# Two-layer pooling, attention and mixture-of-experts backbone on one core: conditioning sections summed by VectorE and GpSimd, tokens loaded first, one load held back

## What is computed

```python
for l in range(DEPTH):                        # DEPTH = 2
    m = jax.nn.silu(c) @ ada_w[l] + ada_b[l]  # ada_w[l] is 1024 x 6144
    sh1, sc1, g1, sh2, sc2, g2 = jnp.split(m, 6, axis=-1)
    if l == 0:                                # the context has a vector of its own
        mc = jax.nn.silu(c_ctx) @ ada_w[l] + ada_b[l]
        hc = modulate(rms_norm(ctx, norm1_g[l]), csh1, csc1)
    h = modulate(rms_norm(x, norm1_g[l]), sh1, sc1)
    if l == 0:
        z = h @ mix_w_in                      # 1024 x 928: pooling | queries | keys
        attn = latent_attention(q, k, v, k_c, v_c)          # 8 heads
        y = concat([multiscale_pool(z), attn]) @ mix_w_out
    else:
        y = conformer_conv(h)
    x = x + g1 * y
    h2 = modulate(rms_norm(x, norm2_g[l]), sh2, sc2)
    x = x + g2 * expert_choice_moe(h2)        # 16 experts, 64 tokens each
return rms_norm(x, final_g)
```

## Time and profile before

| | |
|---|---|
| time of 3 runs | 1566.99 us median (1566.47 to 1567.52) |
| the profiled execution | 1568.4 us, its span 1566.5 us |
| TensorE busy | 1438.4 us, 92% of the span |
| VectorE, ScalarE, GpSimd busy | 27%, 15%, 4% |
| DMA | 501.40 MB, mean 320 GB/s |
| mean granted TensorE clock | 0.971 |

### The profile page before, as it was taken

The page is one execution under the profiler, slowest core; times in us unless marked ns, Lnnn a source line. Parts: engine busy times, 40 slices in busy tenths (PEclk is TensorE's granted clock), DMA queues, the critical chain, the costliest instruction groups (busy, mean ns, idle before and its releaser), DMA issues.

```text
span 1566.5 us, 15305 instructions
## 1 busy us (share of the span) xinstructions
PE 1438.4 (92%) x5889; PEld 597.7 (38%) x5889; DVE 425.6 (27%) x867; ACT 229.5 (15%) x469; POOL 70.2 (4%) x151
## 2 busy tenths in 40 slices
PE   4999999997999899899999999997999998999996
PEld 2564555553333333333323444453433323323332
DVE  2113667333121221121113423535012111111113
ACT  3224333111110010010003112221100100100001
POOL 1000000000000000000000300001000000000001
PEclk7999999997999999999999999998999999999999
DMA  9725686148999999999999103229999999999995
GB/s 348 296 98 185 216 295 241 68 154 316 419 407 420 427 427 429 428 428 428 423 421 369 65 0 128 88 83 364 388 426 396 427 428 428 428 428 428 424 421 212
DMA packets 77234, 501.40 MB, mean 320 GB/s; under 512 B 7624, under 2 KB 8671, under 8 KB 48638
## 3 DMA queue, kind: packets, MB, share of 16 engines
q1 hardware_dynamic: 69952, 485.22, 75.8%
q0 software_dynamic: 2304, 8.39, 1.4%
q10 hardware_dynamic: 4926, 7.04, 1.3%
HBM read 494.32 MB, written 6.31 MB: 320 GB/s over the span
## 4 chain that ended last, share of the span: by engine, by line
PE 70%; DMA 21%; DVE 5%; issue 1%; ACT 1%; ACTq 1%; SPq 0%; POOL 0%; POOLq 0%; DVEq 0%
PE PS L1016 31%; DMA ring<-in_exp_wg_dram 11%; PE PS L814 7%; PE PS L1048 6%; DMA ring<-in_exp_wu_dram 5%; PE PS L733 4%; PE PS L682 4%; PE PS L845 4%; DMA ring<-in_exp_wd_dram 3%; PE PS L653 3%; PE PS L887 3%; PE PS L665 2%; PE PS L908 1%; PE PS L829 1%; PE PS L822 1%
## 5 line engine op out<-in xcount | busy, mean ns | idle before, releaser
L1016 PE MATMUL PS<-ring,arena 128*64 128x512 f32 x2880 | 673.9, 607 | 41.3 <-DMA ring<-in_exp_wg_dram 19.5
L1016 PEld LDWEIGHTS PS<-ring,arena 128*64 128x64 f32 x2880 | 220.4, 139 | 463.2 <-issue 423.6
L1708 DVE TENSOR_TENSOR x<-x,PS 128x512 f32<-128x512 f32 x128 | 87.9, 687 | 466.9 <-PE PS L1048 466.9
L1048 PE MATMUL PS<-arena 128*128 128x512 f32 x256 | 141.5, 641 | 3.7 <-DVE arena L1735 3.2
L814 PE MATMUL PS<-ring,hT 128*128 128x512 f32 x256 | 113.9, 600 | 0.0
L1339 ACT ACTIVATE arena<-PS 128x512 f32<-128x512 f32 x32 | 17.4, 594 | 467.4 <-PE PS L1016 467.4
L1735 DVE SCALAR_TENSOR_TENSOR arena<-PS,arena,g_row 128x512 f32<-128x512 f32 x32 | 22.6, 746 | 219.5 <-PE PS L1016 219.5
L1048 PEld LDWEIGHTS PS<-arena 128*128 128x128 f32 x256 | 38.3, 188 | 105.4 <-issue 97.3
L653 PE MATMUL PS<-ident,arena 128*128 128x128 f32 (+5 forms) x393 | 54.5, 278 | 25.8 <-DVE arena L1726 17.9
L814 PEld LDWEIGHTS PS<-ring,hT 128*128 128x128 f32 x256 | 48.7, 193 | 59.8 <-issue 59.0
L665 PE MATMUL PS<-ring,cond 128*32 128x512 f32 x384 | 51.8, 673 | 14.8 <-DMA ring<-in_ada_w_dram 13.9
(11 more groups left out here) (180 smaller groups left out, 1059.8 us busy)
## 6 DMA issues: line engine op xcount, KB each, us to landing
ring<-in_exp_wg_dram SPq DMA_DIRECT2D x62, 2048.0 KB, 16.1
ring<-in_exp_wd_dram SPq DMA_DIRECT2D x62, 2048.0 KB, 19.2
ring<-in_exp_wu_dram SPq DMA_DIRECT2D x56, 2048.0 KB, 17.9
ring<-in_ada_w_dram SPq DMA_DIRECT2D x24, 2048.0 KB, 9.8
ring<-in_conv_w_pw_dram SPq DMA_DIRECT2D x6, 2048.0 KB, 19.5
hT<-in_exp_wu_dram SPq DMA_DIRECT2D x4, 2048.0 KB, 15.6
ring<-in_mix_w_out_dram SPq DMA_DIRECT2D x2, 2048.0 KB, 16.6
arena<-in_exp_wu_dram SPq DMA_DIRECT2D x2, 2048.0 KB, 7.3
```

Source lines behind the costliest of these rows:

```text
L1016: last = nc.tensor.matmul(PS[64 * e:64 * e + 64, bank + half, :], lhs[:, k, 64 * e:64 * e + 64], w[e][:, half * N:(half + 1) * N], start=k ...
L1048: nc.tensor.matmul(PS[:, 6 + i % 2, :], hot[:, (i // 2) * 128:(i // 2 + 1) * 128], y_rows[:, (i % 2) * N:(i % 2 + 1) * N], start=True, sto ...
L1708: v.tensor_tensor(part, part, PS[:, 6 + i % 2, :], ALU.add).then_inc(scat_added, 1)
```

## The change

Seven things change together.

1. **Tokens first.** SyncE loads x and the context before any granule of `ada_w`; the transposes stand ahead of section 0; small vectors that layer 0's first norm does not need move from ScalarE's queue to SyncE's, behind `mix_w_in` and the pooling tables (the five rows of `params` ahead of `mix_w_in`). The first section waits for two small loads only (`first_bias_in`). `keep_warm(3)` stands before each block of section 1.
2. `cond` holds silu(c) in column 0, silu(c_ctx) in column 16 and zeros elsewhere, instead of 16 copies of each. Column 16 is cleared before attention.
3. **Early sections 2 and 3 on VectorE** (`early_terms`): granules 4 to 7 are no longer multiplied by TensorE; VectorE makes the product and the sum over the eight parts, one `tensor_scalar` and seven `scalar_tensor_tensor` of 128 x 512 per granule, after the items in `SUMMED`. The sum over the 128 partitions is left to the turn and to a `tensor_reduce` over 512 values (`section_total`) in place of 32.
4. Section 2 is turned before the pooling products, in place of after the values.
5. **Half of each late section on GpSimd**: the first granule stays with TensorE, the second is scaled in place by eight `tensor_scalar` (`scale_late`) and summed by seven `tensor_tensor` (`add_late`) into `ada_rows[:, 1]`. A third late slot is used, in turns for the second granules.
6. The loads of one late section are issued together: SyncE waits for the first granule's block of the head before, then issues both.
7. **Held load.** The ninth granule of each mixture also waits for the first gathered rows (`rows_in[0]`), and `keep_warm(6)` becomes `keep_warm(4)`.

Cut to the core:

```diff
+    o = [("xT", (k,), "VS"[k % 2]) for k in range(K8)]
+    o += [("cT", (k,), "VS"[k % 2]) for k in range(K8 // 2)]
+    o += conditioning(0) + conditioning(1)
...
+    o += conditioning(2)[2:]
     o += [("band", (0,), "V"), ("band", (1,), "V"), ("poolw", (0,), "S"), ("poolw", (1,), "S"),
...
+    return o + conditioning(3)[2:]
+SUMMED = {4: ("zlat", 1), 5: ("zlat", 2), 6: ("sel", 2, 1), 7: ("value", 2)}
...
+                    sp.wait_ge(rows_in[0], 16 * (PAIRS // 2 * l + 1))
...
+            for h in range(LATE):
                 for b in range(2):
+                    g = G_LATE + b * (1 + h % 2)
+                    if h < 1 + b:
+                        slot_free(g)
+                    elif b:
+                        sp.wait_ge(late_sum, LATE_STEPS * (h - 1))
+                    else:
+                        sp.wait_ge(late_filled, h)
+                    l, s = divmod(EARLY + h, SECTIONS // 2)
+                    sp.dma_start(slot(g).rearrange("p (k n) -> p k n", k=K8), ada_blocks(l)[s, b, :, :, :])\
+                      .then_inc(slot_in[g % SLOTS], 16)
...
+                    if args[0] in (2, 3):
+                        keep_warm(3)
...
+                    if args[0] in (2, 3):
+                        pe.wait_ge(early_sum, 2 * K8 * (args[0] - 1))
...
             def late_turn(h, half):
                 if half:
                     pe.wait_ge(late_summed, h + 1)
                 else:
+                    pe.wait_ge(late_rows, h + 1)
+                    pe.wait_ge(late_sum, LATE_STEPS * h + LATE_STEPS)
...
             def mixture(l):
-                keep_warm(6)
+                keep_warm(4)
...
+            def early_terms(b):
+                g = GRANULE[("ada", b)]
+                acc = ada_rows[:, b % 2, :]
+                dve.wait_ge(slot_in[g % SLOTS], arrivals(g))
...
+                for k in range(K8):
+                    w = slot(g)[:, k * N:(k + 1) * N]
+                    if k == 0:
+                        v.tensor_scalar(acc, w, cond[:, k, 0:1], None, ALU.mult).then_inc(early_sum, 1)
+                    else:
+                        dve.wait_ge(early_sum, K8 * (b - 4) + k)
+                        v.scalar_tensor_tensor(acc, w, cond[:, k, 0:1], acc, ALU.mult, ALU.add).then_inc(early_sum, 1)
...
+            def scale_late(j, odd):
+                g = G_LATE + 1 + odd
+                pool.wait_ge(slot_in[g % SLOTS], 16 * j + (arrivals(g) - 16 * (LATE // 2 - 1)))
+                for k in range(K8):
+                    w = slot(g)[:, k * N:(k + 1) * N]
+                    p.tensor_scalar(w, w, cond[:, k, 0:1], None, ALU.mult).then_inc(late_sum, 1)
...
+            def add_late(j, odd):
...
+                for k in range(1, K8):
+                    pool.wait_ge(late_sum, LATE_STEPS * h + (K8 + k - 1))
+                    p.tensor_tensor(acc, slot(g)[:, 0:N] if k == 1 else acc, slot(g)[:, k * N:(k + 1) * N], ALU.add)\
+                     .then_inc(late_sum, 1)
...
+            def stage_two_heads(j, late):
+                stage_queries(2 * j)
+                if late:
+                    scale_late(j, 0)
+                stage_keys(j)
                 stage_values(2 * j, 0)
+                if late:
+                    add_late(j, 0)
                 stage_queries(2 * j + 1)
+                if late:
+                    scale_late(j, 1)
                 stage_values(2 * j + 1, 1)
+                if late:
+                    add_late(j, 1)
```

180 lines of the change are left out of this document (93 added, 87 removed).

## The result

The changed kernel takes 1612.53 us (median of 4 runs, 1612.17 to 1614.43) beside 1566.73 us before (4 runs, 1565.04 to 1567.52): ratio 1.0296, 95% interval 1.0280 to 1.0313. The profiled execution took 1614.4 us, span 1612.5. Forecast were 1572.0, at most 1586. The sign was right, the size was not: the loss is 46 us, not 5.

The account below looks back on a forecast made before the run. TensorE was taken to bound 160 to 340 us, DMA 385 to 830, the opening mixed. Terms -2.9 + 0.7 + 14.7 - 6.0 - 1.5 = +5.0 on 1567.0 gave 1572.0 us, range 1558 to 1586.

Parts of the forecast that it names:

- The step that failed: GpSimd's scaling in late heads: 0.67 us per 128 x 512 multiplication, 5.4 for eight; bounds a copy's 0.62 and an addition's 1.31.
- The ring: Attention's late heads: block, pair of loads, GpSimd's scaling, keys' copy, next block; two heads take 42.5 us against 37.9.
- rival 2: GpSimd in attention: a multiplication costs what an addition does, 1.31 us, eight take 10.5; 1596 us in all, chance 0.10.
- the four other terms: Outside attention: opening gains 2.9 us, end of projections loses 0.7, mixtures gain 6.0 and 1.5.
- Opening: Start of kernel: tokens first gains 2.9 us, limited by the second `mix_w_in` granule landing; bounds 0 and 5.
- End of projections: Before attention: loss of 0.7 us, as TensorE's saved blocks are waited away for VectorE's sums; 3.4 lost at first pooling.
- Attention: Late heads: TensorE saves 1.0 us per head, but waits for loads and GpSimd make a loss of 14.7 us.
- Mixtures: Ahead of the mixtures: gain of 6.0 us in layer 0 from earlier rows and higher clock, 1.5 in layer 1.
- Rival 1: Attention: VectorE's divisions and GpSimd's work block each other on the shared port, some 5 us more, 1577; chance 0.13.
- Rival 3: Attention: GpSimd keeps up and keys are never late, -6.0 us in place of +14.7, 1551 us; chance 0.15.
- 4: Rival 4: loads at full rate, multiplications at 0.55 us, attention loses 4, opening's clock kept; 1561 to 1568 us, chance 0.20.

Follow-up runs that it names:

- two_op: Changed kernel with 0.0 added in the same instruction as each GpSimd multiplication: 1578.2 us, ratio 1.0060 against the kernel before.
- keys_first: Changed kernel with the copy of the keys' weights ahead of GpSimd's multiplications: 1595.6 us, ratio 1.0189 against the kernel before.
- te_both: Changed kernel with all early and late sections multiplied by TensorE again; tokens first, zero columns and held load stay: 1554.9 us, ratio 0.9919.
- moved_2: The kernel of moved run once more, in the same rounds as pool_two: 1552.4 us, ratio 0.9897 against the kernel before.
- pool_act: pool_two with the divisions on ScalarE instead of VectorE: 1549.2 us, ratio 0.9891 against the kernel before.
- held: Kernel before with only the held ninth granule and four dummy products instead of six: 1559.3 us, ratio 0.9947.
- pool_two: Changed kernel with second granule loaded a head earlier, keys' weights copied first, early sums placed as in moved, 0.0 added to multiplications: 1558.0 us, ratio 0.9934.
- moved: Changed kernel with late sections back on TensorE and VectorE's early sums placed elsewhere: 1552.3 us, ratio 0.9902 against the kernel before.

## Why the prediction was right or wrong

- **The step that failed**: "I take 0.67, nearest to the copy, since it too reads one tensor". It measured 1.56 at the median and 1.60 in the mean: 12.8 us for eight, not 5.4. Both bounds missed it, the addition's 1.31 too: they took a price for growing with the number of tensors read. It does not (1.49 for one input and a constant, 1.03 for the two-input form, 0.69 with a second operation, 0.61 a copy). The range should have been open above.
- **The ring was right.** For blocks 2 to 4 rival 2 had 9.4 us for 5.1 us more of multiplications per head; by the same measure 42.5 + 9.4 / 5.1 x (12.8 - 5.4) = 56.1, measured 57.8. From two_op to the changed kernel these two heads grow by 13.5 us for 7.0 more of multiplications, 1.9 for each. Over all heads rival 2 gave 24 us for 5.1 us more per head; by the same measure 7.4 us more give 35, so 1607, against 1612.5. With the price put back (two_op) the whole is 1578.2 beside the 1572.0 forecast; 4.7 of these 6 us are attention's.
- **Where the ring sat**: the turns of heads 0, 1 and 5 and the keys of 2 and 4 were named; the longest wait, head 3's turn, came on top. That the keys' waits were in the ring, and not beside it, was seen, but their worth (18 us for a moved copy) only by keys_first.
- **Outside attention luck helped**: the four other terms were forecast at -9.7 together and measured at -9.8, but the opening with the end of the projections came 1.4 worse and the mixtures 1.5 better, so the errors cancelled. All of the miss is attention's: 55.9 in place of 14.7.
- **Opening**: forecast -2.9, measured -4.9. The second `mix_w_in` granule was there at 44.6 (issued 28.1, landed 16.5 later) and its first product at 45.2, near the forecast 45.5; but before, that product stood at 49.1 and not at 48.4, for its eight forerunners took 2.5 us at half clock. The clock rose sooner too, 1.00 from 46 to 48, where before it was still 0.50 from 50 to 52, so the 32 first products took 6.12 us, 7.47 before. The bound of 5 was reached. This is not certain from run to run: in te_both and moved_2, with the same loads ahead, the granule was late and the first projection of a token tile stands at 51.8.
- **End of projections**: forecast +0.7, measured +4.1. The stall at the first pooling product was 3.59 (3.4 forecast). What was left out is the granted clock after each stall: 1.6 us in the pooling row above, 1.0 in the 40 products behind it (5.60 against 4.63 ahead of the stall) and 0.8 in the last turn (1.94 against 1.13), together the 3.4 that the forecast missed; and 1.8 in attention's first products (3.78 against 1.98), counted there.
- **Attention**, TensorE's own gain of 1.0 us per head: two heads 36.1 in pool_act against 37.9, 0.9 each. Right, and never seen in the changed kernel.
- **Mixtures**: forecast -6.0 and -1.5. Measured -5.1 from attention's end to the first product; from there to mixture 1's first product -5.0, of which 2.4 lie between the routing of layer 1 and that product (12.06 to 9.66 us) and 2.6 ahead of it. held gives the same two fives alone. The held granule's effect inside the stage was not in the sum, and its cause stays open. The traces show where the stages part: in the 70 us from 0.5 us behind mixture 0's first product, DMA moved 388 GB/s before at a mean granted clock of 0.97, and 420 GB/s at 1.00 in held.
- **Rival 1** (VectorE and GpSimd block each other): at work, but small here. In attention of the changed kernel the divisions take 0.71 us in the mean instead of 0.63, 3 us in all, and GpSimd's multiplications and additions 2 and 1 us more than their medians make. It grew once GpSimd was busy beside VectorE all the time: pool_two lost to it what TensorE gained. The Trainium skill ("SBUF — State Buffer", section "Who interferes with whom") says that the shared pair is an exclusive lock held for a whole instruction, and that VectorE contends in a two-port `tensor_scalar` and where both inputs lie in SBUF. The runs agree: 0.17 us became 1.23 beside additions of 1.26, and both kinds it names are the ones stretched; copies from PSUM (0.95) and reductions of PSUM (0.95) kept their times.
- **Rival 2** named the right place and slope, with a price too low. **Rival 3** and **4** are refuted for this kernel; rival 3's 1551 is nearly what pool_act reached after five repairs, but by other terms: its attention took as long as before (156.4) and only began earlier, at 124.4.

## What to carry to other kernels

Ahead of moving work to an engine, measure one instruction in exactly its form; neither the number of inputs nor the nearest row bounds its price. Where an in-order queue serves two consumers, look at what each short copy stands behind, and whether its consumer releases the next load: the cost is the ring's. And give a stall of TensorE its second price, the products at half clock that can stand behind it.

## What the hardware showed that was not expected

- GpSimd, 128 x 512 fp32 in place: `tensor_scalar` with one operation 1.56 us (column) or 1.49 to 1.51 (constant, multiplied or added), with two operations (multiply by the column, add 0.0) 0.69, `tensor_tensor` with a broadcast column or the same part twice 1.03, with two different parts 1.26, copy 0.61. Half a row in the single-operation form took 0.92, from which I estimate 0.28 us fixed and 2.5 ns for each element of a row. The Trainium skill ("GPSIMD Engine Reference", section "4.1 Engine selection") calls one-input work "roughly line-rate": the copy and the double operation, both faster than the two-input addition, agree in tendency; the single-operation form does not, and there the measurement decides.
- VectorE beside a busy GpSimd: a 128 x 768 division in SBUF 0.62 us alone, 1.03 in the mean and up to 1.71 beside it; a 0.17 us addition 1.23.
- After idle stretches of 3.6 and 4.2 us TensorE was granted 0.50 (1.2 GHz) for some 4 us or more, and the same four products took 3.75 us instead of 2.13. After 2.22 us it went either way: four products took 3.43 us in moved, 1.98 in moved_2, the same kernel.
- Holding one 2 MB load back until the first rows had been gathered made the kernel before 8 us faster (held). Five are ahead of mixture 0; the profile shows five more from mixture 0's first product to mixture 1's (718.5 to 713.3), where single profiles differ by as much as 6.5 us, and their cause is open.
